# Causal mask added by VectorE in PSUM, and the turned probabilities of full blocks copied by ScalarE

## The chip, the cores and the metric

The kernel runs on one core of one Trainium2 chip. The metric is device time in microseconds (us) of one execution. A difference of less than about 0.2%, some 6.3 us here, can't be told from no change.

## The reference, cut to what matters

The program is a stack of transformer blocks on 512 tokens of width 1024: two layers of (gated feed-forward, a mixer of three kinds of attention, gated feed-forward), then a second block with a dilated attention, a gated recurrence and a mixture of experts. The change touches the causal attention of the two mixers only. For each head and each block of 128 queries it is

```python
s = einsum('bhqd,bhkd->bhqk', qi, k) * scale
s = where(kpos[None, :] <= qpos[:, None], s, -inf)
p = softmax(s, axis=-1)
o = einsum('bhqk,bhkd->bhqd', p, v)
```

Query block i sees key blocks 0 to i, and only the last of them, 128x128, needs the triangular mask.

## The kernel before, in words

The mixer's attention is a list of 16 **pairs** of heads, p0 to p15 (`mixer_pairs`): p0 to p3 have 32 features a head, p4 to p12 have 64, p13 to p15 have 96. Three of them, p4, p7 and p10, attend to 31 compressed keys with a mask of their own. The other 13 are causal (`causal`). Each pair is four **steps**, rows r0 to r3; row ri scores 128 queries of two heads against 128(i+1) keys. A row r3 is a "full block": its `blocks` is `NT` = 4. A layer has 64 steps, the program 128.

All engines run the same list of steps in a software pipeline, written out by hand. Step a does this:

- TensorE (PE), in the order of its queue: `scores(a)` writes two banks of PSUM at L1611 and adds the mask by a product of the identity with a bf16 mask, in the same banks, at L1615. It waits until the exponentials of step a-2 are done, since there are two pairs of score banks. Then `turn(a-3)` transposes the scaled probabilities of step a-3 into banks 2 and 3 (L1624), once the copy of step a-4 has left them. Then `values(a-4)` multiplies the copied, turned probabilities with v (L1639).
- VectorE (DVE): `maximum(a)`, the row maxima straight from PSUM (L2199); `reciprocal(a-1)` of the sums of exponentials (L2204), which waits for ScalarE; `copied(a-3)`, the turned probabilities from PSUM to SBUF (L2212); then, in r0 of some pairs, the result of a pair that has ended (L2221, L2224), and in the steps after p1 and p3 a normalisation (L2241, four times L2249 and L2251).
- ScalarE (ACT): `exp` of step a for both heads, with the sums, at L985; and results and conversions between them.
- GpSimd (POOL): scales the probabilities by the reciprocal and the gate (L753).

Each engine works its queue in order: an instruction that waits holds all behind it. The dilated attention of the second block uses the same functions with `bias` set; its scores have no mask, and its copies are made by ScalarE (L977) already. After the attention of a mixer comes its output projection and the feed-forward, for which all of it must be done. `step(...)` on VectorE is an instruction followed by a wait for its own end.

Of the kernel before, what the change touches and what calls it, by code (L numbers as in the profile page):

```python
# [16 lines left out]
P = 128  # L17
# [153 lines left out]
def program(nc, ffn_w, mix_w, second_w, moe_w, x_in, pos_in, cols_in, rows_in, const_in, const2_in, out):  # L171
# [677 lines left out]
    def _(act):  # L849
# [114 lines left out]
        def attention(pairs, PT, highs=(), behind=None):  # L964
            steps = NT * len(pairs)
            turns, sums = c.at.get(pT_ready.name, 0), c.at.get(pv_ready.name, 0)
            for a in range(steps + VALUES + 9):
                if highs and a in HIGHS_AT:
                    q = highs[HIGHS_AT.index(a)]
                    if q["first"]:  # L970
                        arrived(q["item"])
                    act.activation(q["hi"], q["raw"], ACT.Copy).then_inc(piece_high, 1)
                t = a - TURN
                if 0 <= t < steps and pairs[t // NT]["bias"] is not None:
                    act.wait_ge(pT_ready, turns + 2 * t + 2)
                    act.wait_ge(pv_ready, max(sums + t - 2, 0))
                    act.activation(PT[:, t % 3], banks[:, 2:4], ACT.Copy).then_inc(pT_copied, 1)  # L977
                if a < steps:
                    u, i = pairs[a // NT], row_of(pairs, a)
                    act.wait_ge(max_ready, c.next(max_ready))  # L980
                    act.wait_ge(pT_ready, max(turns + 2 * (a - 3), 0))
                    for e in range(2):
                        n, by = u["tiles"][e][i]["n"], 2 * (a % 4) + e
                        src = PROBS[:, a % 4, e, 0:n] if u["bias"] is not None else SCORES[a % 2][:, e, 0:n]
                        act.activation(PROBS[:, a % 4, e, 0:n], src, ACT.Exp, bias=NM[:, 2 * (a % 2) + e:2 * (a % 2) + e + 1],  # L985
                                       accum_out=DEN[:, by:by + 1]).then_inc(probs_ready, 1)
                if behind and a >= steps:
                    behind(a - steps)
                u = pairs_done(pairs, a, 1)
                if u:  # L990
                    act.wait_ge(pv_ready, sums + NT * (pairs.index(u) + 1))
                    o = bank[4 + u["at"] % 2]
                    if u["bias"] is not None:
                        act.activation(SECOND_HI[u["to"]], o, ACT.Copy).then_inc(o_high, 1)
                    elif u["to"] >= 6:
                        act.wait_ge(o_raw, c.next(o_raw))
                        act.activation(QC[:, u["to"] - 6], KCc[:, u["to"] - 6], ACT.Square).then_inc(o_squared, 1)
                    else:
                        act.activation(MIXED_HI[:, u["to"]], o, ACT.Copy).then_inc(o_high, 1)
                if normed_pairs(pairs, a, 5):  # L1000
                    act.wait_ge(o_mean, c.next(o_mean))
                    act.activation(rms, rms, ACT.Sqrt).then_inc(o_root, 1)
                u = normed_pairs(pairs, a, 10)
                if u:
                    act.wait_ge(o_normed, c.next(o_normed))
                    act.activation(MIXED_HI[:, u["to"]], KCc[:, u["to"] - 6], ACT.Copy).then_inc(o_high, 1)
            c.skip(pT_ready, 2 * steps)
            c.skip(pv_ready, steps)
# [330 lines left out]
    def _(pe):  # L1339
# [252 lines left out]
        def attention(pairs, PT, early=None):  # L1592

            steps = NT * len(pairs)
            exps, maxima, freed = (c.at.get(v.name, 0) for v in (probs_ready, max_ready, o_done))
            copies, means = c.at.get(pT_copied.name, 0), c.at.get(o_mean.name, 0)
            normed = [u["at"] for u in pairs if u["to"] >= 6 and u["last"]]

            def scores(a):
                u, i = pairs[a // NT], row_of(pairs, a)  # L1600
                if u["bias"] is not None:
                    pe.wait_ge(max_ready, max(maxima + a - 1, 0))
                else:
                    pe.wait_ge(probs_ready, max(exps + 2 * (a - 1), 0))
                sides = [t[i] for t in u["tiles"]]
                n, o = sides[0]["n"], SCORES[a % 2]
                wide = 256 if sides[0]["q"].shape[0] <= 64 else T
                for c0 in range(0, n, wide):
                    for e, t in enumerate(sides):
                        c1 = min(c0 + wide, n)  # L1610
                        last = mm(o[:, e, c0:c1], t["q"], t["k"][:, c0:c1], start=c0 == 0, stop=True, skip_group_check=True)  # L1611
                for e, t in enumerate(sides):
                    if t["mask"] is not None:
                        m, at = t["mask"]
                        last = mm(o[:, e, at:at + m.shape[1]], ident16, m, start=False, stop=True, skip_group_check=True)  # L1615
                last.then_inc(scores_ready, 1)

            def turn(a):
                for e in range(2):
                    t = pairs[a // NT]["tiles"][e][row_of(pairs, a)]  # L1620
                    pe.wait_ge(pT_copied, copies + a)
                    pe.wait_ge(scaled_ready, c.next(scaled_ready))
                    for j in range(t["blocks"]):
                        last = nc.tensor.transpose(bank[2 + e][0:t["rows"], P * j:P * j + P],  # L1624
                                                   PROBS[:, a % 4, e, P * j:P * j + t["rows"]], ident)
                    last.then_inc(pT_ready, 1)

            def values(a):
                u, i = pairs[a // NT], row_of(pairs, a)
                t, o = u["tiles"][0][i], bank[4 + u["at"] % 2]  # L1630
                pe.wait_ge(pT_copied, copies + a + 1)
                if u["first"] and a % NT == 0:
                    if u["at"] - 2 in normed:
                        pe.wait_ge(o_mean, means + normed.index(u["at"] - 2) + 1)
                    else:
                        pe.wait_ge(o_done, max(freed + u["at"] - 1, 0))
                for j in range(t["blocks"]):
                    for e in range(2):
                        last = mm(o[64 * e:64 * e + 64, P * i:P * i + P], u["vs"][e][j], PT[0:t["rows"], a % 3, e, P * j:P * j + P],  # L1639
                                  start=u["first"] and a % NT == 0 and j == 0, stop=True, skip_group_check=True)  # L1640
                last.then_inc(pv_ready, 1)

            for a in range(steps + VALUES + 9):
                if a < steps:
                    scores(a)
                if 0 <= a - TURN < steps:
                    turn(a - TURN)
                if 0 <= a - VALUES < steps:
                    values(a - VALUES)
                if early and a - VALUES == steps - 1:  # L1650
                    pe.drain().then_inc(attended, 1)
                if early:
                    early(a)
                u = normed_pairs(pairs, a, 3)
                if u:
                    pe.wait_ge(o_squared, c.next(o_squared))
                    mm(bank[4 + u["at"] % 2], cst(C_BLK, P), QC[:, u["to"] - 6], start=True, stop=True).then_inc(o_sums, 1)
            c.skip(probs_ready, 2 * steps)
            c.skip(max_ready, steps)
            c.skip(pT_copied, steps)  # L1660
            c.skip(o_mean, len(normed))
            c.skip(o_done, 1 + pairs[-1]["at"])
# [219 lines left out]
    def _(dve):  # L1882
# [295 lines left out]
        def attention(pairs, PT, factor=1.0, gain=None, behind=None):  # L2178
# [3 lines left out]
            def maximum(a):  # L2182
# [13 lines left out]
                    step(V.scalar_tensor_tensor(src[:, 1], SCORES[a % 2][:, 1], E_DH ** -0.5, HB[:, 1, at:at + T], ALU.mult, ALU.add))  # L2196
                else:
                    dve.wait_ge(scores_ready, c.next(scores_ready))
                V.tensor_reduce(NM[:, 2 * (a % 2):2 * (a % 2) + 2], src, AX.X, ALU.max, negate=True).then_inc(max_ready, 1)  # L2199

            def reciprocal(a):
# [3 lines left out]

            def copied(a):
                t = pairs[a // NT]["tiles"][0][row_of(pairs, a)]
                if pairs[a // NT]["bias"] is not None:
                    return
                dve.wait_ge(pT_ready, turns + 2 * a + 2)  # L2210
                dve.wait_ge(pv_ready, max(sums + a - 2, 0))
                V.tensor_copy(PT[0:t["rows"], a % 3, :, 0:P * t["blocks"]], banks[0:t["rows"], 2:4, 0:P * t["blocks"]]).then_inc(pT_copied, 1)  # L2212
# [361 lines left out]
```

## Time and profile before

| what | value |
|---|---|
| times of three runs | 3154.17, 3157.39, 3157.86 us (median 3157.39) |
| the profiled execution | 3154.23 us |
| its span, from first to last instruction | 3152.3 us |
| mean granted TensorE clock | 0.97 |
| attention of mixer 0 | 530.7 to about 692 us |
| attention of mixer 1 | 1608.3 to about 1768 us |

The profiled execution's own time is 1.9 us more than its span. The two stretches that the change touches are some 160 us each, about a tenth of the time together. A row of a timeline gives the start, the busy time, the engine, the line and the form of an instruction or of several merged ones ("x8"); the bracket tells how long the engine had been idle, and who released it.

### The profile page before, as it was taken

To read this page: it belongs to the slowest core of one execution; us is meant where nothing else is said; L and a number is where in the kernel's file an instruction comes from. 1 tells how busy PE (TensorE), PEld (TensorE's weight loads), DVE (VectorE), ACT (ScalarE), POOL (GpSimd) and SP (SyncE) were. 2 spreads that over 40 slices of the span, in tenths; PEclk is the share of its full clock that TensorE was granted. 3 is DMA by queue.
4 is the path that set the end of the run, shared out by engine and by line. 5 is a ranking of instruction groups with operands and counts; after the bars stand their busy time and mean duration, and the time that the engine had idled before them with its cause. 6 is when DMAs were issued, how large, how long until landed. Compare 5 with 4: busy or idle time off the path is not lost.

```text
span 3152.3 us, 42555 instructions
## 1 busy us (share of the span) xinstructions
PE 2944.7 (93%) x16264; PEld 2236.0 (71%) x16264; DVE 1829.1 (58%) x2565; ACT 915.3 (29%) x1656; POOL 1141.4 (36%) x662
## 2 busy tenths in 40 slices
PE   6999999999999999999999999999997577998988
PEld 5888867677888878887676778887795466554443
DVE  6766684757655676667767565667527975111111
ACT  3222232543222232223235422223236542111111
POOL 4444354444434444443544443443333650000000
PEclk9999998999999999999999999999999788999999
DMA  5222222013222222221300222222230004999998
GB/s 186 96 100 100 80 81 81 1 37 113 91 100 100 80 101 100 99 87 74 116 26 2 77 104 100 100 84 94 80 121 14 7 1 165 412 417 417 417 417 343
DMA packets 58468, 411.46 MB, mean 131 GB/s; under 512 B 6480, under 2 KB 6736, under 8 KB 25424
## 3 DMA queue, kind: packets, MB, share of 16 engines
q1 hardware_dynamic: 58176, 408.02, 33.6%
q8 instruction: 103, 1.69, 0.2%
q0 software_dynamic: 144, 1.38, 0.1%
q14 instruction: 45, 0.37, 0.0%
HBM read 407.28 MB, written 2.10 MB: 130 GB/s over the span
## 4 chain that ended last, share of the span: by engine, by line
PE 74%; DVE 11%; DMA 7%; ACT 3%; issue 3%; SPq 1%; POOL 1%; DVEq 0%; ACTq 0%; POOLq 0%
PE banks L1564 9%; PE banks L1563 9%; PE banks L1562 9%; DMA experts<-moe_w 6%; PE banks L1527 5%; PE banks L1396 5%; PE banks L1573 5%; PE banks L1574 5%; PE banks L1575 5%; PE banks L1833 4%; PE banks L1475 3%; PE banks L1611 3%; PE banks L1844 2%; PE banks L1639 2%; PE banks L1624 2%
## 5 line engine op out<-in xcount | busy, mean ns | idle before, releaser
L762 POOL TENSOR_TENSOR ffn_parts<-ring,ffn_parts 128x2048 fp32r<-128x2048 f32 x88 | 407.7, 4634 | 739.9 <-ACT ffn_parts L858 739.9
L2137 DVE SCALAR_TENSOR_TENSOR x<-banks,x 128x512 f32<-128x512 f32 x704 | 474.5, 691 | 304.4 <-PE banks L1575 304.1
L1833 PE MATMUL banks<-experts,mix 128*64 128x256 f32 x2048 | 254.5, 392 | 35.3 <-DMA experts<-moe_w 35.3
L1562 PE MATMUL banks<-x_parts_low,ffn_parts 128*128 128x512 f32 x672 | 264.3, 393 | 0.0
L1564 PE MATMUL banks<-x_parts_high,ffn_parts 128*128 128x512 f32 x672 | 264.3, 393 | 0.0
L1563 PE MATMUL banks<-x_parts_high,ffn_parts 128*128 128x512 f32 x672 | 264.1, 393 | 0.0
L1562 PE MATMUL banks<-h_lo,ffn_parts 128*128 128x512 f32 x672 | 262.2, 390 | 0.0
L1564 PE MATMUL banks<-h_hi,ffn_parts 128*128 128x512 f32 x672 | 261.4, 389 | 0.0
L1563 PE MATMUL banks<-h_hi,ffn_parts 128*128 128x512 f32 x672 | 261.4, 389 | 0.0
L858 ACT ACTIVATE ffn_parts<-ring 128x2048 fp32r<-128x2048 f32 x88 | 168.6, 1916 | 296.2 <-PE banks L1564 289.7
L767 POOL TENSOR_TENSOR ffn_parts<-ring,ffn_parts 128x1024 fp32r<-128x1024 f32 x88 | 212.7, 2418 | 104.6 <-ACT ffn_parts L862 104.5
L1833 PEld LDWEIGHTS banks<-experts,mix 128*64 128x64 f32 x2048 | 143.0, 140 | 143.0 <-DMA experts<-moe_w 53.0
L2461 DVE SCALAR_TENSOR_TENSOR late<-banks,late 128x128 f32<-128x128 f32 x64 | 22.3, 349 | 291.5 <-ACT late L1323 291.5
L931 ACT ACTIVATE mix<-mix 128x512 f32<-128x512 f32 x88 | 55.6, 632 | 444.8 <-DVE mix L2122 444.8
L862 ACT ACTIVATE ffn_parts<-ring 128x1024 fp32r<-128x1024 f32 x88 | 93.4, 1061 | 304.7 <-PE banks L1575 304.7
L985 ACT ACTIVATE probs<-banks,small 128x256 f32<-128x256 f32 (+4 forms) x256 | 120.5, 478 | 147.5 <-DVE small L2199 147.4
L1573 PE MATMUL banks<-ffn_parts 128*128 128x512 f32 x352 | 139.0, 395 | 9.5 <-DVE x L2137 4.8
L1563 PEld LDWEIGHTS banks<-x_parts_high,ffn_parts 128*128 128x128 f32 x672 | 126.2, 188 | 29.8 <-issue 0.5
L1562 PEld LDWEIGHTS banks<-x_parts_low,ffn_parts 128*128 128x128 f32 x672 | 126.0, 188 | 29.6 <-issue 0.5
L1573 PE MATMUL banks<-ffn_hidden,ffn_parts 128*128 128x512 f32 x352 | 139.9, 397 | 7.3 <-issue 4.4
L1564 PEld LDWEIGHTS banks<-x_parts_high,ffn_parts 128*128 128x128 f32 x672 | 126.2, 188 | 28.5
L1562 PEld LDWEIGHTS banks<-h_lo,ffn_parts 128*128 128x128 f32 x672 | 126.1, 188 | 26.8 <-issue 0.5
(383 smaller groups left out, 6508.7 us busy)
## 6 DMA issues: line engine op xcount, KB each, us to landing
ring<-ffn_w SPq DMA_DIRECT2D x88, 1536.0 KB, 6.6
experts<-moe_w SPq DMA_DIRECT2D x128, 1024.0 KB, 18.4
experts<-moe_w SPq DMA_DIRECT2D x128, 512.0 KB, 17.8
ring<-mix_w SPq DMA_DIRECT2D x24, 1536.0 KB, 6.6
ring<-second_w SPq DMA_DIRECT2D x16, 1536.0 KB, 6.5
x<-x_in SPq DMA_DIRECT2D x8, 256.0 KB, 8.0
out<-x SPq DMA_DIRECT2D x8, 256.0 KB, 3.0
table<-const_in POOLq DMA_DIRECT2D x1, 1344.0 KB, 11.0
```

The lines of the kernel that those rows point to most:

```text
L762: pool.tensor_tensor(s[:, 1], w, s[:, 0].bitcast(F32), ALU.subtract).then_inc(up_split, 1)
L767: pool.tensor_tensor(s[:, 1], w, s[:, 0].bitcast(F32), ALU.subtract).then_inc(down_split, 1)
L858: act.activation(W_UP[:, n % 2, 0], ring[:, (base + n) % SLOTS, 0:2048], ACT.Copy).then_inc(w_high, 1)
L1396: last = mm(bank[n % 4][0:j["rows"], 0:j["n"]], w, r, start=k == 0, stop=k == len(j["terms"]) - 1)
L1527: last = mm(o, w, r, start=k == 0, stop=k == len(j["terms"]) - 1)
L1562: mm(bank[n % 2 + 2 * a], w[:, 0, a, k], lo[:, k], start=k == 0, stop=False)
L1563: mm(bank[n % 2 + 2 * a], w[:, 0, a, k], hi[:, k], start=False, stop=False)
L1564: last = mm(bank[n % 2 + 2 * a], w[:, 1, a, k], hi[:, k], start=False, stop=k == KC - 1)
L1573: mm(bank[4 + q % 4], w[:, 0, P * q:P * q + P], g[:, 1], start=True, stop=False)
L1574: mm(bank[4 + q % 4], w[:, 0, P * q:P * q + P], g[:, 0], start=False, stop=False)
L1833: last = mm(o, XIN[:, k, P * p + 64 * e:P * p + 64 * e + 64], w[:, k], start=k == 0, stop=k == KC - 1, skip_group_check=True)
L2137: V.scalar_tensor_tensor(x[:, q], bank[4 + q % 4], scale, x[:, q], ALU.mult, ALU.add).then_inc(down_used, c.one(down_used))
```

## The change

In the 13 causal pairs of each mixer, TensorE no longer adds the mask. VectorE adds the triangle (the float32 constant `C_TRI`, the same for both heads) to the last 128 columns of both score banks in place, waits for the end of that, and then takes the maxima. The compressed pairs (`rows` = 31) keep TensorE's product. In the full blocks (r3) of the causal pairs, ScalarE makes the copy of the turned probabilities in place of VectorE; in its queue the copy of step a-3 stands before the exponentials of step a. The other rows, and the compressed pairs, keep VectorE's copy. The dilated attention, all of whose blocks are full, runs as before.

```diff
 # scalar: attention
                 t = a - TURN
-                if 0 <= t < steps and pairs[t // NT]["bias"] is not None:
+                if 0 <= t < steps and pairs[t // NT]["tiles"][0][row_of(pairs, t)]["blocks"] == NT:
                     act.wait_ge(pT_ready, turns + 2 * t + 2)
                     act.wait_ge(pv_ready, max(sums + t - 2, 0))
                     act.activation(PT[:, t % 3], banks[:, 2:4], ACT.Copy).then_inc(pT_copied, 1)
 # tensor: scores
-                    if t["mask"] is not None:
+                    if t["mask"] is not None and t["rows"] < P:
                         m, at = t["mask"]
 # vector: maximum
                     dve.wait_ge(scores_ready, c.next(scores_ready))
+                    if u["tiles"][0][i]["rows"] == P:
+                        last = src[:, :, n - P:n]
+                        step(V.tensor_tensor(last, last, cst(C_TRI, P).unsqueeze(1).to_broadcast([P, 2, P]), ALU.add))
                 V.tensor_reduce(NM[:, 2 * (a % 2):2 * (a % 2) + 2], src, AX.X, ALU.max, negate=True).then_inc(max_ready, 1)
 # vector: copied
-                if pairs[a // NT]["bias"] is not None:
+                if pairs[a // NT]["bias"] is not None or t["blocks"] == NT:
                     return
```

## Rows read from the trace of the kernel before

**Rows 1.** Busy time by stretch: mixer 0's attention, its opening, mixer 1's opening.
```profile
530.00:692.00 162.00, 152.96 (x1328) 105.93 (x1329) 109.50 (x220) 78.61 (x274) 75.40 (x131) 0.95 0.01 1
...
530.00:533.00 3.00, 1.56 (x12) 0.85 (x12) 1.57 (x3) 0.76 (x4) 0.00 (x0) 0.93 0.00 0
533.00:536.00 3.00, 2.90 (x14) 2.15 (x16) 1.11 (x4) 1.07 (x5) 0.72 (x2) 0.50 0.00 0
...
1611.00:1621.00 10.00, 9.77 (x52) 6.04 (x50) 4.76 (x11) 4.88 (x19) 4.81 (x10) 0.51 0.00 0
```

**Rows 2.** Waits in the attention of mixer 0: engine and line, for whom, us, times.
```profile
ACT probs L985 <- DVE small L2199: 74.4, 45, 3.5
DVE small L2199 <- PE banks L1615: 32.1, 36, 2.0
...
PEld banks L1624 <- DVE ring L2212: 9.5, 16, 1.2
```

**Rows 3.** Timeline of an ordinary pair, p2 into p3.
```profile
553.84 0.70 PE L1611 MATMUL banks<-mix 32*128 32x256 f32 x4
...
553.90 0.69 DVE L2212 COPY ring<-banks 128x512 f32<-128x512 f32 x1
...
554.64 0.87 PE L1624 MATMUL banks<-const,probs 128*128 128x128 f32 x6
554.79 0.69 DVE L2199 TENSOR_REDUCE small<-banks 128x2 f32<-128x512 f32 x1 [0.21 <-PE banks L1615]
...
558.79 1.13 PE L1611 MATMUL banks<-mix 32*128 32x256 f32 x8
559.86 0.28 PE L1615 MATMUL banks<-mask 128*128 128x128 bf16 x2
559.98 0.39 PE L1624 MATMUL banks<-const,probs 128*128 128x128 f32 x2
560.18 1.23 DVE L2199 TENSOR_REDUCE small<-banks 128x2 f32<-128x1024 f32 x1 [0.82 <-PE banks L1615]
...
562.93 0.70 PE L1611 MATMUL banks<-mix 32*128 32x256 f32 x4
```

**Rows 4.** Timeline in the dilated attention: VectorE's chain and ScalarE's copy.
```profile
2389.42 0.67 DVE L2195 SCALAR_TENSOR_TENSOR probs<-banks,mix 128x512 f32<-128x512 f32 x1
...
2390.00 0.68 DVE L2196 SCALAR_TENSOR_TENSOR probs<-banks,mix 128x512 f32<-128x512 f32 x1
...
2390.72 1.22 DVE L2199 TENSOR_REDUCE small<-probs 128x2 f32<-128x1024 f32 x1
...
2390.89 1.00 ACT L977 ACTIVATE ring<-banks 128x1024 f32<-128x1024 f32 x1
```

**Rows 5.** Timeline of r3 of p13, with 96 features.
```profile
657.12 1.98 PE L1611 MATMUL banks<-mix 96*128 96x512 f32 x4
...
659.26 1.22 DVE L2199 TENSOR_REDUCE small<-banks 128x2 f32<-128x1024 f32 x1 [1.56 <-PE banks L1615]
```

**Rows 6.** Timeline of r0 of p8, where the result of p6 is taken.
```profile
608.50 0.49 PE L1611 MATMUL banks<-mix 64*128 64x128 f32 x4
...
609.25 0.42 DVE L2199 TENSOR_REDUCE small<-banks 128x2 f32<-128x256 f32 x1 [1.05 <-PE banks L1615]
```

**Rows 7.** Timeline of p10, a compressed pair: the full copy of p9.
```profile
630.57 1.22 DVE L2212 COPY ring<-banks 128x1024 f32<-128x1024 f32 x1 [0.77 <-PE banks L1624]
...
631.85 0.41 PE L1624 MATMUL banks<-const,probs 128*31 128x128 f32 x2
```

**Rows 8.** VectorE's normalisation after p1 and p3, grouped by line.
```profile
L2249 DVE RECIPROCAL rms<-rms 128x128 f32<-128x128 f32 x8 | 7.5, 942 | 0.0
```

**Rows 9.** Timeline of both mixers: first r1, and mixer 1's r1 of p2.
```profile
531.41 0.70 PE L1611 MATMUL banks<-mix 32*128 32x256 f32 x4
...
1609.00 0.70 PE L1611 MATMUL banks<-mix 32*128 32x256 f32 x4
...
1628.51 0.70 PE L1611 MATMUL banks<-mix 32*128 32x256 f32 x4
```

## The prediction

> **What bounds the kernel now.** I read first the page's shares, to place the change: both attentions together are a tenth of the span, so the question is what sets the pace inside them. The busy times by stretch [rows 1] show TensorE busy for 152.96 of 162 us in mixer 0, VectorE for 109.50, ScalarE for 78.61; mixer 1 is like it. That seems to say TensorE, and that taking work from it helps. But a matmul row's end is modelled, and TensorE here often runs one step's work while another chain is what ends last. So I went on to the waits [rows 2]: ScalarE waits 74.4 us for maxima, VectorE's maxima wait 32.1 us for the mask product, and TensorE's transposes wait 9.5 us for VectorE's copies. The three hand work round in a circle. The chain of waits in order of time names, in nearly every pair, the same stations: scores of r1, r2, r3 on TensorE, maxima of r3 on VectorE, exponentials of r3 on ScalarE, scores of the next r1.
>
> An ordinary pair [rows 3] is therefore two links. From the scores of r1 at 553.84 to those of r3 at 558.79 TensorE sets the pace: 4.95 us. From r3 at 558.79 to the next r1 at 562.93 it is the chain of the softmax: 4.14 us, of which 1.39 pass until the maxima start at 560.18, and 2.75 in maxima and exponentials. The period is 9.09 us.
>
> **The add.** No row shows VectorE writing PSUM, nor an add of 2x128 columns. Nearest are the maxima over 128x256 at 0.42 [rows 6]; and an operation of 512 columns takes 0.69 and one of 1024 1.22 [rows 3, 4], so 512 columns more cost 0.53, and 256 fewer save 0.27, which again gives 0.42. To it comes the wait for its own end: in the dilated attention the maxima start 0.72 after an operation of 0.68 that is waited for, so 0.04 more [rows 4]. I take 0.45 to 0.46 from the start of the add to the start of the maxima. The bounds: without the wait the next operation starts 0.58 after one of 0.67 (2389.42 to 2390.00), 0.09 early, hence 0.33 from below; from above, that a write to PSUM costs as much as the form twice as wide, 0.69 plus 0.04, hence 0.73.
>
> The Trainium skill, "VectorE: DVE Perf Modes", section "The DRAIN you can't avoid", holds that the flush of the pipe stands between two operations anyway, so that a semaphore costs nothing extra. The trace doesn't agree: 0.72 with the wait, 0.58 without, for the same form. By that rule the add would be 0.33, and the sum below about 5 us lower.
>
> **TensorE without the masks.** In r3, the mask starts at 559.86 and the transpose behind it at 559.98 [rows 3]: a mask takes 0.12 of TensorE's queue, and no more, although the row reads 0.28. Over the 104 masked steps of both mixers that is 12.5 us, the most that TensorE can gain.
>
> **Link two, r3 to the next r1.** Scores end 1.13 after their start, 0.04 passes to VectorE, 0.45 is the add: the maxima start at 1.62 in place of 1.39, so +0.23. In the pairs with 96 features the scores end at 1.98, so 2.47 in place of 659.26 - 657.12 = 2.14 [rows 5]: +0.33.
>
> **Link one, r1 to r3.** The mask of r1 gives nothing back: the transpose at 554.64 starts 0.05 after VectorE's copy ends (553.90 + 0.69) [rows 3], so the copy holds it. The mask of r2 gives 0.12. The maxima of r1 start 0.24 later (554.54 + 0.04 + 0.45 against 554.79), and with them the copy that the next transpose needs; TensorE is there 0.09 later than it, so this is hidden, by a thin cover. Link one: -0.12.
>
> **The copy.** ScalarE's takes 1.00 [rows 4], VectorE's 1.22. In an ordinary pair both end before TensorE needs it, and VectorE waits 0.82 for r3's scores after its copy, so taking it away gives nothing there. ScalarE makes it before the exponentials of r2, which then start some 0.5 us later; the scores two steps on, which wait for them, have 0.7 of room. Behind a compressed pair's short steps the copy is on the path: VectorE's copy starts when the transposes are done, at 630.57, it takes 1.22, and the next transpose starts 0.06 after it, at 631.85 [rows 7]. With ScalarE's 1.00 that is 631.62: -0.23.
>
> **Sum for one mixer**, link by link:
> - plain pairs p2, p9, p12: 3 x (0.23 - 0.12) = +0.33.
> - p3: VectorE copies a result of 512 columns (0.69, as the copy of that width) before r1's maxima, so the copy that r2's transposes need is behind add and result and is late by 0.22; with link two: +0.45.
> - p4 to p6: the normalisation, with four reciprocals of 0.94 [rows 8] and more, fills VectorE's queue. It loses 1.22 and gains three adds, 1.36; walked through: +0.07.
> - p6 to p8: it loses 1.22 and gains two adds, 0.9; and ScalarE's copy ends 0.2 earlier: -0.43.
> - p8 and p11: the result of a pair waits for the exponentials of r0 and stands before r1's maxima. The maxima of r0 start 0.98 after the scores in place of 0.75 [rows 6], r1's add comes on top, 0.45, and link two's 0.23: 2 x 0.91 = +1.82.
> - p10: ScalarE's copy, -0.23.
> - p13 to p15: link two 3 x 0.33; only p13 gets both masks of link one back, -0.24, since in the others the result holds the copy: +0.75.
> - the opening, at half the clock: masks give twice as much, less the adds of r0 and r3: -0.15.
>
> Together +2.6, for two mixers +5.2 us. All that follows waits for the attention and shifts by as much. On the profiled execution, 3154.2 (span 3152.3 and 1.9 around it), that gives 3159.4. That execution lies 3.2 below the median of the runs; the four times of before lie in twos around 3154.2 and 3157.6. I lay the sum on the middle, 3155.9, and forecast 3161.
>
> Some 20 adds of a mixer are on the path (13 of r3, 7 of r0 and r1 in the pairs with results): each 0.1 on the add is 4 us on the time. The bounds 0.33 and 0.73 give 3156 and 3172.
>
> **Rivals.**
> 1. *VectorE becomes what holds the transposes* (slower). The cover of 0.09 in link one is gone once the add takes over 0.54; then each copy of r2 is late too. For it: that cover, and the unknown write to PSUM. Against: every VectorE row here goes by its width. At 0.73 for each add: 3172.
> 2. *The masks are gained in full* (faster). If the transposes of r1 aren't held by copies, link one gives 0.41 in place of 0.12, and VectorE's lost 1.22 gives 0.4 to the four stretches behind p6 and p10: 20 x (0.23 - 0.41) + 6 x 0.09 - 4 x 0.4 = -4.7: 3151. Against: the copy's end 0.05 before the transpose.
> 3. *The clock* (slower). Its lower level of 1.2 GHz (0.50) holds from 533 on, after a stretch with TensorE busy 1.56 of 3 us, and from 1611 to 1621 in mixer 1 [rows 1]. From the first r1 to p2's r1 mixer 0 needs 22.4 us (531.41 to 553.84) and mixer 1 19.5 [rows 3, 9]: its longer half-rate stretch costs 2.9. TensorE with fewer products and the same waits could fall into one more: 3164. The Trainium skill, "TensorE: Matmul & The Clock Gate", section "What's actually happening", says that a monitor of recent activity sets the clock, which speaks against taking products away.
> 4. *ScalarE's copy does nothing or harm* (slower). If exponentials of r2, 0.5 later, hold scores two steps on, where normalisation steps and table loads have used up the 0.7 of room: 0.3 in 20 pairs, 3167.
>
> **Chances.** The forecast 0.50 (own range 3156 to 3166); rival 1 0.20; rival 2 0.14; rival 3 0.10; rival 4 0.06. The range 3152 to 3170 leaves out most of rival 1's far end and half of rival 2. The 6 us that a measurement can tell cut the forecast in two: a third of it lies above. Faster 0.06 (rival 2's far side), within 0.2% 0.50, slower 0.44 (0.17 of the forecast, nearly all of rivals 1 and 4, half of 3).
>
> **What the profile after would show.** Adds of 0.42, maxima 0.45 after them. The maxima of r3 start 1.62 after r3's scores in pairs with 32 and 64 features, 2.47 with 96. The period from r1 to r1 in plain pairs 9.20. Behind p9 the next transposes start 0.23 sooner after the full ones. VectorE busy 22 us more in a mixer for 52 adds, less 16 for 13 copies; ScalarE 13 more. Each mixer 2.6 longer by the same two instructions. The prediction is wrong if adds take over 0.54, if transposes of r2 start later than 3.17 after r1's scores in plain pairs, or if the half-rate stretches change in number.

## The result and the profile after

The changed kernel takes 3175.22 us (median of 9 runs, 3164.71 to 3180.28), the kernel before 3155.66 beside it (9 runs, 3152.04 to 3157.86). The ratio is 1.0060, with a 95% interval of 1.0048 to 1.0072: slower, by 19.6 us. The forecast was 3161, its range 3152 to 3170. The direction was right and the size was not, and most of the missing part is TensorE's clock.

The profiled execution after took 3179.51 us, span 3177.7, mean granted clock 0.962 (before: 3154.23, 3152.3, 0.970). These two executions are 25.3 us apart, more than the medians. First the busy time by stretch of the changed kernel, to be laid beside [rows 1]; the columns are PE, PEld, DVE, ACT and POOL busy (instructions), then the granted clock, DMA share and GB/s:

```profile
530.00:692.00 162.00, 147.65 (x1134) 99.32 (x1136) 111.29 (x250) 86.55 (x277) 70.41 (x125) 0.85 0.01 1
549.00:563.00 14.00, 14.00 (x76) 9.65 (x74) 7.28 (x15) 3.85 (x15) 4.19 (x8) 0.50 0.01 1
592.00:604.00 12.00, 11.78 (x52) 6.20 (x50) 7.71 (x18) 7.00 (x16) 5.49 (x8) 0.50 0.00 0
```

In 162 us from 530 on the granted clock was 0.95 before and is 0.85 now. Before, the level 0.50 (1.2 GHz) ended between 549 and 550 in this mixer. Now it goes on to 564, and comes back from about 591 to 605 and from 629 to 632; in mixer 1 the stretches are about 1626 to 1643, 1680 to 1684, 1697 to 1704, 1711 to 1721 and 1745 to 1748. Note how the row of a half-rate stretch reads: TensorE "busy" 14.00 of 14, and about half the instructions of the same 14 us before, which were nearly all at full clock:

```profile
549.00:563.00 14.00, 13.88 (x144) 9.81 (x140) 9.35 (x19) 5.96 (x21) 5.60 (x10) 0.98 0.00 1
```

Next the waits in mixer 0, engine and line, for whom, us, times, longest, to be laid beside [rows 2]:

```profile
ACT probs L985 <- DVE small L2202: 57.3, 38, 4.4
DVE banks L2201 <- PE banks L1611: 37.5, 28, 3.9
...
PEld banks L1624 <- DVE ring L2215: 20.4, 30, 1.9
...
PE banks L1624 <- DVE ring L2215: 12.1, 21, 1.7
```

TensorE's transposes wait more for VectorE's copies: 20.4 us in the weight loads in place of 9.5, 12.1 in the products in place of 7.0. The weight load and the product often wait for one and the same copy, so the sum, 32.5 in place of 16.5, serves to compare kernels and is not idle time: TensorE's products stand idle 14.4 of the 162 us in place of 9.0. The groups of the new instructions in the same mixer, by form (busy us, mean ns of one, idle before them):

```profile
L2201 DVE TENSOR_TENSOR banks<-banks,const 128x256 f32<-128x256 f32 x52 | 22.2, 428 | 37.7 <-PE banks L1611 37.5
...
L977 ACT ACTIVATE ring<-banks 128x1024 f32<-128x1024 f32 x12 | 12.3, 1023 | 20.4 <-PE banks L1624 20.4
```

And the timeline of r3 of p9 into p10, at full clock:

```profile
634.70 1.13 PE L1611 MATMUL banks<-mix 64*128 64x256 f32 x8
...
635.88 0.43 DVE L2201 TENSOR_TENSOR banks<-banks,const 128x256 f32<-128x256 f32 x1 [1.39 <-PE banks L1611]
...
636.34 1.22 DVE L2202 TENSOR_REDUCE small<-banks 128x2 f32<-128x1024 f32 x1
...
637.60 0.69 ACT L985 ACTIVATE probs<-banks,small 128x512 f32<-128x512 f32 x1 [1.46 <-DVE small L2202]
...
639.10 0.41 PE L1611 MATMUL banks<-mix 64*128 64x31 f32 x4
```

The add takes 0.43 and the maxima start 0.46 after it; they stand 1.64 after the scores (forecast 1.62), and from r3's scores to those of the next r1 are 4.40 us (forecast 4.14 + 0.23). So where the clock is full, the steps are as they were worked out. The time went where it is not.

### The profile page after: what moved, and what is told of

Read it like the earlier page. It is cut to its first block, busy times and chain, and to the rows that moved or that the text cites. A ratio compares the mean times of both kernels' runs of the same rounds, so it can differ in the third digit from the quotient of the medians.

```text
span 3177.7 us, 42243 instructions
## 1 busy us (share of the span) xinstructions
PE 2959.9 (93%) x16056; PEld 2241.8 (71%) x16056; DVE 1840.8 (58%) x2643; ACT 940.3 (30%) x1682; POOL 1142.9 (36%) x662
## 4 chain that ended last, share of the span: by engine, by line
PE 73%; DVE 12%; DMA 7%; issue 3%; ACT 3%; SPq 1%; POOL 1%; DVEq 0%; ACTq 0%; POOLq 0%
PE banks L1563 9%; PE banks L1564 9%; PE banks L1562 9%; DMA experts<-moe_w 6%; PE banks L1527 5%; PE banks L1396 5%; PE banks L1573 5%; PE banks L1574 5%; PE banks L1575 5%; PE banks L1833 4%; PE banks L1475 3%; PE banks L1611 3%; PE banks L1624 2%; PE banks L1844 2%; PE banks L1639 2%
## 5 line engine op out<-in xcount | busy, mean ns | idle before, releaser
L1624 PE MATMUL banks<-const,probs 128*128 128x128 f32 (+1 forms) x696 | 119.4, 307 | 35.4 <-DVE ring L2215 24.3
L1611 PE MATMUL banks<-mix 64*128 64x256 f32 (+7 forms) x800 | 141.0, 425 | 11.6 <-ACT probs L985 4.1
```

## Where the 19.6 us went

**Two measures.** The half-rate time of a profiled execution: in stretches of 4 us over both attentions, twice the missing part of the granted clock, summed; it is the time that TensorE spent at 0.50. Before it is 17.0 in mixer 0 and 13.6 in mixer 1, 31 in all, in three stretches; after it is 47.8 and 41.0, 89 in all, in eight. And the length from the maxima of one r3 to those of the next, pair by pair, since that is the period of the pipeline. The same pair shows what the level costs. The maxima of r3 of p1 and p2 in the changed kernel, in mixer 0, where the half-rate stretch lies over them, and in mixer 1, where it does not:

```profile
551.03 1.22 DVE L2202 TENSOR_REDUCE small<-banks 128x2 f32<-128x1024 f32 x1
...
565.66 1.22 DVE L2202 TENSOR_REDUCE small<-banks 128x2 f32<-128x1024 f32 x1
...
1643.85 1.22 DVE L2202 TENSOR_REDUCE small<-banks 128x2 f32<-128x1024 f32 x1
...
1653.13 1.22 DVE L2202 TENSOR_REDUCE small<-banks 128x2 f32<-128x1024 f32 x1
```

It took 14.63 us against 9.28, for the same instructions; before, the pair took 9.10. That is 5.35 us for some 13 at half rate, 0.41 for each.

**The structure.** Pairs that ran at full clock in both kernels give the part of the change that is not the clock: +0.18 (p2 and p12), +0.52 (p3), +0.11 (p6), +0.80 (p8), +0.78 (p11), +0.12 (p13), +0.37 (p14, p15). With p9 taken like p12 that is 3.6 us a mixer, 7 for both. p5 ran partly at half rate in both mixers (+1.24 in mixer 1, with 3.4 us at half rate) and is not in the sum. From the start of mixer 0's attention to the last r3 maxima of mixer 1, the profiled executions grew by 29 us, 4 more than the whole span did, so the loss lies there: 7 us are structure, and 58 us more at half rate stand beside the rest.

**The clock.** Over repeated runs of the kernel before, the time falls by 2.0 to 2.4 us for each 0.001 of mean granted clock (three groups of 15 to 21 runs, 0.967 to 0.973), over the 9 of the changed kernel by 2.4 (0.961 to 0.967). The mean clock is 0.9697 before and 0.9629 after: 0.0068 lower, 14 to 16 of the 19.6 us, if the slope within one kernel holds between the two. That leaves 4 to 6 for the structure; by the pairs it was 7, which leaves 12 to 13 for the clock. So the clock is 12 to 16 of the 19.6.

## The experiments

Three theories stand in the expectations. C: the clock, in two variants, that TensorE lost products, or that it waits longer for VectorE's copies and so does less in the same time. S: the chain, each add of 0.45 on it. K: ScalarE's copy holds its exponentials. All ratios are against the kernel before, run beside: its median was 3155.66 beside the changed kernel, 3154.33 beside e1 to e4, 3156.39 beside e5 to e8 and 3155.37 beside e9 to e11, and its mean clock is taken over the 56 runs of the last three groups. The half-rate time is of one profiled execution each, and the same kernel varies in it; the clock is the mean over all its runs.

| kernel | median us (runs) | ratio, 95% interval | half-rate us | mean clock |
|---|---|---|---|---|
| before | 3155.66 (9) | 1 | 31 | 0.9697 |
| changed | 3175.22 (9) | 1.0060, 1.0048 to 1.0072 | 89 | 0.9629 |
| e1 add only | 3187.46 (4) | 1.0102, 1.0081 to 1.0123 | 99 | 0.9612 |
| e2 copies only | 3149.40 (10) | 0.9985, 0.9975 to 0.9995 | 27 | 0.9700 |
| e3 changed, 1 product a head | 3169.69 (6) | 1.0046, 1.0033 to 1.0060 | 79 | 0.9663 |
| e4 before, operation added | 3187.10 (4) | 1.0102, 1.0081 to 1.0123 | 72 | 0.9642 |
| e5 before, masks left out | 3153.50 (11) | 0.9994, 0.9984 to 1.0003 | 58 | 0.9663 |
| e6 changed, r3's mask by TensorE | 3161.51 (11) | 1.0019, 1.0010 to 1.0028 | 65 | 0.9668 |
| e7 changed, 4 products a head | 3178.26 (5) | 1.0073, 1.0059 to 1.0087 | 34 | 0.9708 |
| e8 copies, 4 products a head | 3172.15 (5) | 1.0055, 1.0042 to 1.0069 | 21 | 0.9732 |
| e9 changed, r2's copies moved too | 3174.84 (6) | 1.0060, 1.0046 to 1.0074 | 96 | 0.9622 |
| e10 copies of r2 and r3 only | 3148.52 (11) | 0.9981, 0.9972 to 0.9990 | 38 | 0.9712 |
| e11 copies, 4 products in p0 | 3147.10 (8) | 0.9974, 0.9964 to 0.9984 | 27 | 0.9718 |

### The two halves of the change: e1 and e2

e1 takes the change of the mask alone, VectorE keeps all copies (the two edits of the copies are taken back). e2 is the opposite:

```diff
 # e1: mask by VectorE, copies as before
-if 0 <= t < steps and pairs[t // NT]["tiles"][0][row_of(pairs, t)]["blocks"] == NT:
+if 0 <= t < steps and pairs[t // NT]["bias"] is not None:
 # e2: copies as changed, masks as before
-if t["mask"] is not None and t["rows"] < P:
+if t["mask"] is not None:
```

> The mask part alone: VectorE adds the triangle, all copies stay with VectorE. Clock theory (C: with fewer products TensorE drops to half rate more often; that is most of the 19.6 us): nearly all of the loss is here, +14 to +22 us against before, and the half-rate time of the two attentions is 60 us or more in place of 30.7. Chain theory (S: the adds on the path of the softmax cost what was lost, some 0.23 to 0.9 a pair): +6 to +9 us, and no more half-rate time than before. Copy theory (K: ScalarE's copy delays the exponentials and costs most of it): +5 us or less.

> The copy part alone: masks by TensorE as before, full blocks copied by ScalarE. C and S: between -4 and +1 us, half-rate time as before (15 to 35 us). K: +10 us or more.

The mask alone costs 33 us, the copies alone give 5 back. With the add in place the copies are worth more, 12 us (3187.5 against 3175.2). In e2 the mean clock is that of before, and the period of the pairs at full clock shows where the 5 us come from: p3 to p5 17.10 in place of 18.22, p5 to p6 9.14 in place of 10.18, p6 to p8 and p9 to p11 0.19 less, plain pairs 9.10 as before. That is 2.5 a mixer, nearly all where VectorE also normalises. K is refuted: no pair at full clock is longer with ScalarE's copy.

### The operation without the lost products: e4, and the lost products without the operation: e5

e4 is the kernel before with all of TensorE's masks, and an operation of VectorE of the add's size that multiplies by one, waited for. e5 is the kernel before without the causal masks, and nothing in their place.

```diff
 # e4, in maximum(a)
+if u["tiles"][0][i]["rows"] == P:
+    last = src[:, :, n - P:n]
+    step(V.tensor_tensor(last, last, ones.unsqueeze(1).to_broadcast([P, 2, P]), ALU.mult))
 # e5, in scores(a)
-if t["mask"] is not None:
+if t["mask"] is not None and t["rows"] < P:
```

> The kernel before, with TensorE's masks kept and one more VectorE operation in place on the last 128 columns before the maxima (a multiplication by one, 128x256, waited for like the add). TensorE's products are all there, the chain is longer by 0.46 in every masked step. C with lost products: no more half-rate time than before, 20 to 40 us, and +8 to +12 us (0.46 in place of 0.23 in each link). C with waits as the cause: half-rate time of 60 us or more and +20 us or more. S: +8 to +12 us.

> The kernel before, with TensorE's mask products left out in the causal pairs and nothing in their place: the causal mask is not applied, so the output isn't the reference's. It does one half of the mask's move alone, the taking away, with no add on VectorE. Lost products set the clock: half-rate time of the two attentions (about 31 us before, 99 with VectorE's adds, 72 with adds while the products stay) rises to 60 or more, and the time, which could fall by at most 12.5 us, ends at 3150 to 3165. Longer waits set the clock: the half-rate time stays within 10 us of 31, and what is left is the structure, link one's 0.12 and link two's shorter queue: -3 to -8 us, 3147 to 3153. Structure alone, no part of the clock: the same -3 to -8.

The windows of the two attentions in e4:

```profile
530.00:700.00 170.00, 153.54 (x1274) 103.06 (x1274) 127.27 (x267) 78.59 (x274) 74.24 (x129) 0.90 0.00 1
1607.00:1785.00 178.00, 162.10 (x1281) 110.95 (x1281) 129.10 (x267) 75.39 (x262) 72.82 (x125) 0.89 0.02 8
```

and TensorE's waits for the copies in its mixer 0:

```profile
PEld banks L1624 <- DVE ring L2215: 17.4, 25, 1.6
PE banks L1624 <- DVE ring L2215: 13.2, 22, 1.4
```

With every product kept, the clock still falls to 0.90 and 0.89, and the waits for copies grow from 16.5 to 30.6 us (17.4 + 13.2). So an operation on VectorE that adds nothing to and takes nothing from TensorE brings half-rate stretches. The clock isn't all of its 33 us, though: 0.0055 lower is 11 to 13. The rest is structure, more than the 8 to 12 of S, since p3 (+0.73), p5 to p6 (+1.14) and p9 to p11 (+1.41) grew more at full clock than a plain pair. The windows of e5:

```profile
530.00:700.00 170.00, 158.60 (x1289) 111.25 (x1290) 114.04 (x224) 83.36 (x281) 80.10 (x133) 0.95 0.03 11
1607.00:1785.00 178.00, 168.80 (x1285) 117.86 (x1282) 115.22 (x223) 84.06 (x276) 81.36 (x132) 0.89 0.04 13
```

The lost products alone bring them too: not in the profiled execution's mixer 0, but in mixer 1, where the first stretch goes from 1605 on to 1636 and p1 to p2 takes 14.51 in place of 8.82; its half-rate time is 58 us in all. Both variants of C hold, and in the mean clock they add up: 0.0034 lower by the lost products (e5), 0.0055 by the operation (e4), 0.0085 by both (e1).

The two say, too, what removing the products was worth. At full clock 0.28 in a plain pair (8.82 against 9.10), 7 us if all 26 gave as much: but the time fell by only 2.9, and the interval holds no change. With the operation in place it was worth nothing at all: e1 takes 3187.5 and e4 3187.1, e4 with the longer pairs and e1 with the lower clock. The operation itself costs 0.47 in a plain pair (9.57), all of it on the chain of r3, as S says; the two give 0.47 - 0.28 = 0.19 where the changed kernel shows 0.18.

### One link of four: e6

```diff
 # scores(a)
-if t["mask"] is not None and t["rows"] < P:
+if t["mask"] is not None and (t["rows"] < P or t["blocks"] == NT):
 # maximum(a)
-if u["tiles"][0][i]["rows"] == P:
+if u["tiles"][0][i]["rows"] == P and u["tiles"][0][i]["blocks"] < NT:
```

> The changed kernel, but in full blocks (r3) the mask stays a product of TensorE and VectorE adds none; r0 to r2 keep the add, ScalarE keeps its copies. Structure: link two is that of before again, which takes back 0.23 in 20 pairs and 0.33 in 6: 6.6 us, 3168.6. Longer waits set the clock: a quarter of the adds gone, and these the ones after which TensorE waits longest, so the half-rate time falls from 89 us to between 50 and 75, some 4 to 10 us more in time: 3159 to 3165. Lost products set the clock: a quarter of them back, in the rows with most work anyway: half-rate 75 to 85, 3166.

A quarter of the adds carries some 14 of the 19.6 us. Structure alone would have given 3168.6 and the lost products alone 3166; the measured 3161.5 and 65 us of half rate lie inside what the clock with waits gives. Plain pairs take 9.03, less than before's 9.10: the adds of r0 to r2 are indeed hidden, and TensorE gets the masks of r1 and r2 back. Even so the kernel is 5 us slower than before, which the clock, still 0.003 lower, accounts for.

### Giving TensorE something to do: e3, e7, e8 and e11

Products whose result nobody reads, into the bank that the transposes are about to fill, behind the wait for the copy: one a head (e3), four a head (e7) in the changed kernel, four a head with the copies alone (e8), and the same in the steps of p0 only (e11).

```diff
 pe.wait_ge(pT_copied, copies + a)
+if t["rows"] == P and pairs[a // NT]["bias"] is None:     # e11: and a < NT
+    for _ in range(4):                                    # e3: once
+        mm(bank[2 + e][:, 0:P], ident16, tri16, start=True, stop=True)
 pe.wait_ge(scaled_ready, c.next(scaled_ready))
```

> The changed kernel with as many bf16 128x128x128 products as were removed, put in front of the transposes of the causal pairs, into banks 2 and 3 that the transposes then overwrite; the output is the same. TensorE's work is restored, its place is not in the chain from scores to maxima. C with lost products as the cause: half-rate time back to 20 to 40 us, and +4 to +8 us against before. C with longer waits of TensorE as the cause: half-rate time stays over 60 us, +15 us or more. S: as the changed kernel or slower, +18 to +25 us.

> The changed kernel, and in every causal step four more bf16 products of 128 columns a head, whose result nobody reads, between TensorE's wait for the copy and its wait for the scaled probabilities; one a head gave 3169.7. Eight products by 0.06 are 0.48 us of TensorE a step. If the clock follows how much TensorE does, the half-rate time falls from 79 us (one a head) to 40 or less, and at least 10 us come back, less what of the 0.48 is on the path: 3155 to 3168. If it follows the waits between products that a filler behind the wait doesn't shorten, the half-rate time stays at 70 or more and the fillers cost 0.1 to 0.4 in most of 52 steps a mixer: 3175 to 3205.

> TensorE's masks as before, ScalarE's copies of full blocks as in the change (which alone gave 3149.4 against 3154.3), and the same four products more a head in every causal step. The two attentions have about 31 us at half rate. If more work of TensorE keeps the clock up: half-rate 15 or less, 8 us back, and the fillers' 0.48 partly hidden: 3142 to 3155. If not, the fillers' cost in the steps that TensorE paces (link one, 4.95 us of 9.09): 0.5 to 1 us a pair, 3165 to 3180.

> TensorE's masks as before, ScalarE's copies of full blocks, and four products a head that nobody reads in the four steps of p0's transposes only. With such products in all pairs the first half-rate stretch of mixer 0 ended some 10 us sooner and the opening was 2.4 us shorter, while each plain pair at full clock was 1.1 to 1.8 longer. If the opening alone can be had: 2 us less than with the copies alone in mixer 0 and 0 to 2 in mixer 1, 3145 to 3148. If the stretch comes later instead, as in mixer 1 with products in all pairs: 3149 to 3153.

e3 puts back as many products as the change took. 5.5 us come back (4.2 against the kernel before run beside each; the two intervals overlap) and 10 of the 89 us at half rate. The mean clock rises by 0.0034, as much as e5 lost by taking the products away, but a plain pair takes 9.45 in place of 9.28. The half-rate time stays where the variant with waits had put it, over 60. e7 settles that the granted clock follows how much TensorE does. The windows of e7 where the changed kernel stood at 0.50, from 549 to 563 and around 597:

```profile
549.00:563.00 14.00, 14.00 (x162) 10.49 (x160) 10.78 (x23) 7.64 (x25) 6.40 (x12) 1.00 0.01 1
590.00:604.00 14.00, 13.97 (x147) 10.26 (x144) 12.47 (x25) 9.27 (x23) 5.44 (x9) 0.92 0.00 1
```

The half-rate time is back to 34 us, near the 31 of before, and the clock is 0.001 above that of before; e8 reaches 21 us and 0.9732. But the products cost more than the clock gives back: of the 1.92 us a pair that they were put at (four steps of 0.48), 0.95 shows in a plain pair of e7 (10.23 against 9.28), and 1.55 and 1.09 in e8 (10.65 in p2 and 10.19 in p9, against 9.10). The time is worse in both, and for e7 it lies above the 3168 that was the most expected with the clock restored. Work for the clock's sake is worth it only where it costs less than 0.4 us for each us of half rate that it spares. e11 tries the cheapest place. In mixer 0 the half-rate time fell from 17.0 to 13.7, but p0 to p1 took 13.83 as against 13.74 in e2, so the opening gained nothing there; in mixer 1 it rose from 10.2 to 13.6, with 13.93 for p0 to p1 as against 11.20. The 3147.1 can't be told from e2's 3149.4, whose intervals overlap.

### More off VectorE: e9 and e10

```diff
 # ScalarE's and VectorE's conditions, and ScalarE's width
-"blocks"] == NT
+"blocks"] >= 3
-act.activation(PT[:, t % 3], banks[:, 2:4], ACT.Copy)
+act.activation(PT[:, t % 3, :, 0:wide], banks[:, 2:4, 0:wide], ACT.Copy)   # wide = P * blocks
```

> The changed kernel, and the copies of r2 (three blocks, 0.95 us on VectorE) made by ScalarE too. It takes work off VectorE and nothing from or to TensorE: of VectorE's copies that TensorE waits for (32.5 us of waits in mixer 0 after the change, 16.5 before) a further part goes. Longer waits set the clock: the half-rate time of the two attentions falls from 89 us to 70 or less and the time by 5 to 10 us, to 3165 to 3170, if ScalarE has room. Only the number of products sets it: half-rate stays at 85 to 95 and the time within 3 us of 3175. ScalarE, which now copies ahead of the exponentials of two rows of four, becomes what is waited for: over 3178.

> The kernel before, with the copies of r2 and r3 made by ScalarE and the masks left with TensorE. ScalarE's copy of r3 alone gave back 2.5 us a mixer, all of it in the stretches from p3 to p6 where VectorE also normalises, 0.19 behind p6 and p9, and nothing in plain pairs. If VectorE's queue is still the limit there: 1 us a mixer more, 3147. If it is not, the same as with r3 alone, 3149 to 3151. If ScalarE's exponentials are now late: a plain pair over 9.10, 0.3 or more in each of 18, 3155 or more.

e9 brought nothing: the same time as the changed kernel, half-rate 96 us. The reason stands in its waits for VectorE's copies (the lines of this kernel are one further down):

```profile
PEld banks L1625 <- DVE ring L2216: 16.4, 24, 1.9
...
PE banks L1625 <- DVE ring L2216: 10.5, 19, 1.7
```

26.9 of the 32.5 us of waits are still there: TensorE waits for the copies of the short steps, r0, r1 and the compressed pairs, which are all that VectorE still makes here, and little for that of r2. So it didn't take the wait away, and tells little between the variants of C. At full clock some pairs did get shorter (p3 by 0.34, p6 to p8 by 0.5, p14 and p15 by 0.26 each), and the time shows none of it. e10 is within 1 us of e2: p6 to p8 is 0.53 better than there, p3 to p6 1.4 worse.

e2, e10 and e11 are the versions that beat both kernels, by 5 to 8 us against before. Their intervals leave out 1, but only just: the gain of e2 and e10 is below the 0.2% that was set at the start.

## Why the prediction was wrong

**The failed step: the clock.** Rival 3 said that "TensorE with fewer products and the same waits could fall into one more", for 2.9 us and a chance of 0.10, and the sum left the clock as it was. Both halves of that sentence were off. The waits were not the same. The recorded ones doubled, from 16.5 to 32.5 us. And not one stretch more came but, in the profiled execution, five, with a longer first one in both mixers: 58 us more at half rate. By the medians the clock is 12 to 16 us of the 19.6. The price was fair: 2.9 us for a first stretch that is 6.9 us longer in mixer 0 than in mixer 1 (17.1 against 10.2) is 0.42 for each us, and a whole pair shows 0.41. The amount was wrong, some 7 us in place of 58.

**What I should have seen.** I walked the stretch from p4 to p6 for its length alone and found +0.07. Where it ran at full clock its length is near that: 0.11 more from p5 to p6, and 0.20 less from the scores of p4's r1 to the transposes below. But inside it TensorE's work fell and its idle time rose, and that the length hides. TensorE and VectorE in p5 of the changed kernel, ahead of the stretch at half rate that begins at about 591.3:

```profile
588.63 0.92 PE L1611 MATMUL banks<-mix 64*128 64x256 f32 x8
589.37 0.35 DVE L2254 SCALAR_TENSOR_TENSOR mix<-mix,cols,rms 128x128 f32<-128x128 f32 x1
589.64 0.42 DVE L2201 TENSOR_TENSOR banks<-banks,const 128x256 f32<-128x256 f32 x1
590.10 0.69 DVE L2202 TENSOR_REDUCE small<-banks 128x2 f32<-128x512 f32 x1
...
590.78 0.39 DVE L2215 COPY ring<-banks 31x256 f32<-31x256 f32 x1
...
591.22 0.57 PE L1624 MATMUL banks<-const,probs 128*31 128x128 f32 x2 [1.67 <-DVE ring L2215]
```

The copy of 31 rows, for which TensorE stands idle 1.67 us, waits behind the add and the maxima of r1. The same transposes waited 0.98 in the kernel before:

```profile
585.41 0.41 PE L1624 MATMUL banks<-const,probs 128*31 128x128 f32 x2 [0.98 <-DVE ring L2212]
```

From the scores of p4's r1 to these transposes, the same steps in both kernels and all at full clock, TensorE is busy 9.68 of 12.12 us, against 10.22 of 12.32 before: it is idle 2.44 in place of 2.10. The clock falls just after the wait of 1.67. First the row of the changed kernel:

```profile
579.10:591.22 12.12, 9.68 (x98) 6.80 (x98) 10.78 (x28) 8.25 (x27) 4.73 (x11) 1.00 0.01 2
```

and that of the kernel before:

```profile
573.09:585.41 12.32, 10.22 (x105) 7.14 (x105) 11.04 (x27) 7.34 (x26) 4.74 (x11) 1.00 0.01 2
```

The Trainium skill, "TensorE: Matmul & The Clock Gate", section "What's actually happening", lets the recent activity of TensorE set the clock; e5, e7 and e8 agree, and e4 adds that a slower neighbour does it while TensorE keeps all its products. I cited it and gave it 0.10.

**Point by point.**
- The add: forecast 0.42 and 0.45 to the maxima; 0.43 and 0.46. Both bounds, 0.33 and 0.73, fell away, and rival 1 with the upper one. Rival 1's 3172 lies closest to the result, but nothing of its mechanism is there: the transposes in step r2 start 3.06 after r1's scores in p12 (655.49 to 658.55), and it was to show by more than 3.17. That this bound came nearest is chance.
- Link two: forecast +0.23, 4.40 - 4.14 = 0.26 measured. Link one: forecast -0.12; p12's is 4.89 in place of 4.95, -0.06. Hence 0.18 to 0.20 in a plain pair in place of 0.11, and p13 to p15 0.86 in place of 0.75.
- p3: +0.45 forecast, +0.52. p10 and p11 together: -0.23 + 0.91 = 0.68 forecast, 0.78. p6 to p8: -0.43 + 0.91 = 0.48 forecast, 0.80, the term that was off most; what holds it was not tried.
- The copy: ScalarE's 1.02; after the compressed pair's full copy the next transposes start 1.11 after the copy does (642.96 to 644.07) in place of 1.28, -0.17 where -0.23 stood. Rival 4 is refuted by e2.
- The opening: -0.15 forecast. In both mixers it is the longer half-rate stretch that counts: +2.8 from p0 to p1 in mixer 1, +5.5 from p1 to p2 in mixer 0.
- The sum of the structure: 5.2 forecast, 4 to 7 measured.
- Busy times: VectorE's adds 22.2 us in a mixer (forecast 22), ScalarE's copies 12.3 in 12 recorded ones (forecast 13). "The prediction is wrong if the half-rate stretches change in number": they did.

**What stays open.** That less work of TensorE for the same time brings the stretches is shown; which pair falls into one, isn't to be said ahead: p1 to p2 ran at half rate in mixer 0 and not in mixer 1, with the same instructions. And the times of the changed kernel spread over 16 us in 9 runs; those of before spread over 6 in 9, and over 9 to 12 in the groups of 15 to 21.

## What to carry to other kernels

Where TensorE works in a ring with other engines, taking work from it and giving a smaller amount to its neighbour lowers its activity twice: by the work itself and by the longer wait for the neighbour. Set up TensorE's busy and idle time for the same steps before and after, not only the length of the path; where it loses work on both counts and the trace already has half-rate stretches nearby, work out the sum once with pairs at their half-rate length too (here +5.35 us on 9.28), and give that case more than a tail's chance.

An edit of two parts is best priced apart: here the copies, thought of as the lesser part, were worth 5 us alone and 12 beside the add, and the mask's move cost 33. The part worth keeping was the small one: it takes work off VectorE, and nearly all its gain lies where VectorE also normalises.

## What the runs showed of the hardware

- VectorE writing 128x256 in place in PSUM takes 0.43 us, as reading 128x256 from it does for the maxima (0.42), and the next operation starts 0.46 after one that is waited for.
- A stretch at half rate shows TensorE as fully busy: 14.00 of 14 us with 76 products, where 13.88 held 144 before, and the same scores of r3 take 2.08 in place of 1.13 [rows 3]. TensorE's busy share thus rises there while it does less. The row of p1's r3 at half rate, with 32 features as the one in [rows 3]:

```profile
548.44 2.08 PE L1611 MATMUL banks<-mix 32*128 32x256 f32 x8
```

- Taking the 208 mask products away alone cost 0.0034 of the mean clock, and gave 2.9 us, within the noise, where the pairs at full clock promised 7.
- Each 0.001 of mean granted clock is 2.0 to 2.4 us of this kernel's time, over repeated runs of one and the same kernel.
